# Branch gates by one tanh on ScalarE in place of exponential, addition and reciprocal, with the convolution tables copied in the input projections

## What is computed

```
h    = rms_norm(x) * (1 + scale) + shift
proj = h @ w_in                      # hy_u, hy_z, q, k, v, at_z, pl_u, pl_z, mg
y_hy = hyena_branch(hy_u) * silu(hy_z)       # 2 long convolutions, by DFT tables
y_at = diff_attention(q, k, v) * silu(at_z)  # 4 heads, 2 softmax maps in each
y_pl = pool_branch(pl_u) * silu(pl_z)
r    = sigmoid(mg)                   # 3 x 1024 channels
merged = r[0]*(y_hy @ w_hy_o) + r[1]*(y_at @ w_at_o) + r[2]*(y_pl @ w_pl_o)
x    = x + gate * (merged @ w_out)
```

## Time and profile before

| | us |
|---|---|
| median of three executions | 4487.88 |
| lowest, highest | 4482.55, 4494.41 |
| profiled execution, own time | 4486.91 |
| profiled execution, span of the core | 4485.2 |
| TensorE busy in the span | 3701.7 (83%) |
| VectorE busy | 2068.0 (46%) |
| ScalarE busy | 1068.8 (24%) |
| GpSimd busy | 775.1 (17%) |
| mean granted clock of TensorE | 0.913 |

### The profile page before, as it was taken

How to read it: one execution, slowest core, us unless ns; L and a number is a source line. 1 busy time by engine, 2 the same in 40 slices (tenths; PEclk the granted TensorE clock), 3 DMA queues, 4 the chain that set the end, 5 groups by cost and what they waited for, 6 DMA issues and landing times. The chain is left out here.

```text
span 4485.2 us, 53438 instructions
## 1 busy us (share of the span) xinstructions
PE 3701.7 (83%) x19456; PEld 3371.2 (75%) x19456; DVE 2068.0 (46%) x2294; ACT 1068.8 (24%) x1695; POOL 775.1 (17%) x390
## 2 busy tenths in 40 slices
PE   6988849997975877877998679988858787788999
PEld 6766639986764777777998679876647777778989
DVE  3444343222554676674333243234537667663332
ACT  1233321221111332332121121211113333331221
POOL 1112011220221111111111122202111111101211
PEclk9988969999887998999999889998879898899999
DMA  4656652212665221211333442125572122113334
GB/s 131 213 192 194 193 207 80 70 73 76 237 235 179 68 73 49 67 51 65 108 103 110 160 158 80 54 96 199 205 248 70 55 66 70 51 35 109 104 111 144
DMA packets 216869, 537.21 MB, mean 120 GB/s; under 512 B 37172, under 2 KB 78005, under 8 KB 215894
## 3 DMA queue, kind: packets, MB, share of 16 engines
q1 hardware_dynamic: 204214, 474.94, 31.3%
q10 hardware_dynamic: 12544, 60.82, 4.1%
HBM read 390.23 MB, written 165.17 MB: 124 GB/s over the span
## 5 line engine op out<-in xcount | busy, mean ns | idle before, releaser
L1753 PE MATMUL ps<-hh,attn_fwh 128*128 128x384 f32 x1152 | 430.2, 373 | 16.8 <-DMA hl<-h_keep 11.1
L1753 PE MATMUL ps<-hh,attn_fwl 128*128 128x384 f32 x1152 | 409.3, 355 | 0.0
L1753 PE MATMUL ps<-hl,attn_fwh 128*128 128x384 f32 x1152 | 408.0, 354 | 0.0
L2080 DVE RECIPROCAL attn_fout<-attn_fout 128x384 f32<-128x384 f32 x144 | 367.6, 2553 | 5.0
L1931 ACT ACTIVATE attn_prob<-ps,attn_nmax 128x1280 f32<-128x1280 f32 x144 | 176.0, 1222 | 527.4 <-DVE attn_nmax L2085 527.4
L127 PE MATMUL ps<-hh,mixin_wh 128*128 128x384 f32 x720 | 167.0, 340 | 102.3 <-POOL mixin_wl L1134 97.0
L1753 PEld LDWEIGHTS ps<-hh,attn_fwh 128*128 128x128 f32 x1152 | 233.3, 202 | 24.1 <-DMA hl<-h_keep 11.9
L1794 PE MATMUL ps<-ident,attn_prob 128*128 128x128 f32 x648 | 115.8, 294 | 161.2 <-DVE attn_wl L2105 91.8
L1753 PEld LDWEIGHTS ps<-hl,attn_fwh 128*128 128x128 f32 x1152 | 233.9, 203 | 0.0
L2007 POOL TENSOR_TENSOR attn_fwl<-attn_fraw,attn_fwh 128x1024 fp32r<-128x1024 f32 x48 | 121.4, 2530 | 649.0 <-ACT attn_fwh L1898 649.0
L1753 PEld LDWEIGHTS ps<-hh,attn_fwl 128*128 128x128 f32 x1152 | 232.6, 202 | 0.0
(11 more groups left out here) (264 smaller groups left out, 8762.7 us busy)
## 6 DMA issues: line engine op xcount, KB each, us to landing
gates<-attn_fout SPq DMA_DIRECT2D x144, 192.0 KB, 1.9
branch_gate<-gates SPq DMA_DIRECT2D x48, 576.0 KB, 3.8
H_dram<-fspec_hout SPq DMA_DIRECT2D x100, 256.0 KB
fspec_araw<-in_w_ada SPq DMA_DIRECT2D x48, 512.0 KB, 4.1
conv_hs<-H_dram SPq DMA_DIRECT2D x32, 768.0 KB, 5.6
attn_fraw<-in_w_mg ACTq DMA_DIRECT2D x48, 512.0 KB, 3.3
w_in_raw<-in_w_in SPq DMA_DIRECT2D x44, 512.0 KB, 3.9
fspec_draw<-in_dft_taps SPq DMA_DIRECT2D x68, 256.0 KB, 3.4
```

The lines of the kernel that those rows point to most:

```text
L1753: last = pe.matmul(ps[:, X_BANK, 0:CH], w[:, j % 2, k, :], x[:, k, (c % 3) * CH:(c % 3 + 1) * CH], start=(k == 0 and n == 0), stop=(k == K ...
L2080: dve.reciprocal(fout[:, c % 2], fout[:, c % 2]).then_inc(S["fr"], 1)
```

## The change

In attention `gate_out` computes tanh(x / 2) instead of exp(−x), and `sigmoid`, which made 1 / (1 + exp(−x)) of it, is gone from VectorE with its two semaphores; `store_gate` waits for ScalarE's activation. As sigmoid(x) = (1 + tanh(x / 2)) / 2, `branches_out` adds 1 to the gate in the same instruction that multiplies it with the product, and the factor of a half is put into the output stage's gate column.

The 32 table copies are taken out of the filters. `mixers_in` issues them from ScalarE's queue, two for each of 16 tiles: behind the eviction of tiles 0 to 11, and for the four pooling tiles directly behind `ready`. As `mixers_in` runs in each layer, there are 64 copies instead of 32. SyncE waits for them at the end of `mixers_in`, and `long_conv` no longer waits.

```diff
 def filters(...)
                         spectrum_out(m)
-                        if s % 2:
-                            i = n * 8 + s // 2
-                            name = ("dft_fwd", "dft_inv")[i // 16]
-                            act.dma_start(tables[name][i % 16], A[name][i % 16]).then_inc(s_tab, 16)
...
 def mixers_in(...)
                 sp.wait_ge(S["wv"], 16)
+                sp.wait_ge(S["tab"], 16 * 32)
...
+                def keep_table(i):
+                    for name in ("dft_fwd", "dft_inv"):
+                        act.dma_start(tables[name][i], A[name][i]).then_inc(S["tab"], 16)
...
                         evict_hy(2 * i + b, b)
+                        keep_table(2 * i + b)
                 for t in (10, 11):
                     ready(t)
                     split(t % 2, 6 * 16)
                     evict_hy(t, t % 2)
+                    keep_table(t)
...
                 for g in range(4):
                     ready(20 + g)
+                    keep_table(12 + g)
                     if g < 2:
                         split(g, 11 * 16)
...
 def long_conv(...)
-                sp.wait_ge(s_tab, 16 * 32)
...
 def attention(...)
                 def store_gate(h, c):
-                    sp.wait_ge(S["fr"], NCH * h + c + 1)
+                    sp.wait_ge(S["fev"], NCH * h + c + 2)
...
-                    nc.scalar.activation(fout[:, c % 2], ps[:, X_BANK, 0:CH], ACT.Exp, scale=-1.0).then_inc(S["fev"], 1)
+                    nc.scalar.activation(fout[:, c % 2], ps[:, X_BANK, 0:CH], ACT.Tanh, scale=0.5).then_inc(S["fev"], 1)
...
-                def sigmoid(h, c):
-                    q = NCH * h + c
-                    dve.wait_ge(S["fev"], q + 2)
-                    dve.tensor_scalar(fout[:, c % 2], fout[:, c % 2], 1.0, None, ALU.add).then_inc(S["fone"], 1)
-                    dve.wait_ge(S["fone"], q + 1)
-                    dve.reciprocal(fout[:, c % 2], fout[:, c % 2]).then_inc(S["fr"], 1)
...
                         low(h, u - 1, 0)
-                        sigmoid(h, cs[0])
                         maximum(h, u, 1)
                         low(h, u - 1, 1)
                         low(h, u - 1, 2)
                         combine(h, u)
-                        if u not in PV_OF:
-                            sigmoid(h, cs[1])
...
 def branches_out(...)
-                            dve.tensor_tensor(three(gate[:, b]), banks(b)[:, :, 0:CH], three(gate[:, b]),
-                                              ALU.mult).then_inc(S["p"], 1)
+                            dve.scalar_tensor_tensor(out=three(gate[:, b]), in0=three(gate[:, b]), scalar=1.0,
+                                                     in1=banks(b)[:, :, 0:CH], op0=ALU.add, op1=ALU.mult
+                                                     ).then_inc(S["p"], 1)
...
 def output(...)
-                        dve.tensor_copy(g, mod[:, bass.ds(2 * KD + m, 1), :].rearrange("p a n -> p (a n)")
-                                        ).then_inc(S["gc"], 1)
+                        dve.tensor_scalar(g, mod[:, bass.ds(2 * KD + m, 1), :].rearrange("p a n -> p (a n)"), 0.5, None,
+                                          ALU.mult).then_inc(S["gc"], 1)
```

More of the change, by code:

```diff
@@ L170, in build @@
         tables = {n: scratch(f"{n}_kept", [16, 2, P, BR]) for n in ("dft_fwd", "dft_inv")}
-        s_tab = top.enter_context(nc.semaphore("h_tab"))
         with phase(nc, "start") as ph:
@@ L182, in build @@
         mods = keep("mods", [P, DEPTH, 24, 2])
-        filters(nc, A, ps, mods, ident, x_state, H_dram, Hp_dram, hinv, tables, s_tab)
+        filters(nc, A, ps, mods, ident, x_state, H_dram, Hp_dram, hinv)
         with nc.Fori(0, DEPTH) as l:
@@ L192, in build @@
                 wv = hctx.enter_context(nc.sbuf_tensor("w_v_raw", [P, KD, BR], F32))
-                mixers_in(nc, A, l, ps, pr, ident, hh, hl, raw, wv, mix, qk)
+                mixers_in(nc, A, l, ps, pr, ident, hh, hl, raw, wv, mix, qk, tables)
                 values(nc, A, O, l, ps, hh, hl, wv, mix, v, vrows, s_kept)
             with nc.Fori(0, 2) as o:
-                long_conv(nc, A, l, o, ps, ident, v, mix, H_dram, Hp_dram, hinv, tables, s_tab)
+                long_conv(nc, A, l, o, ps, ident, v, mix, H_dram, Hp_dram, hinv, tables)
             vctx.close()
@@ L221, in reduce_and_sin, with filters @@
     return dve.tensor_scalar(ang, ang, PI_IN, -PI_IN, ALU.min, ALU.max)
-def filters(nc, A, ps, mods, ident, x_state, H_dram, Hp_dram, hinv, tables, s_tab):
+def filters(nc, A, ps, mods, ident, x_state, H_dram, Hp_dram, hinv):
     NU, NS = UNITS_F, TILES_F
@@ L877, with mixers_in @@
 WHY = NT + 4
-def mixers_in(nc, A, l, ps, pr, ident, hh, hl, raw, wv, mix, qk):
+def mixers_in(nc, A, l, ps, pr, ident, hh, hl, raw, wv, mix, qk, tables):
     with phase(nc, "mixin") as ph:
@@ L910, in mixers_in @@
                  "rot", "rused", "sp6", "spread", "qr", "cos", "sh0", "sh1", "pm", "pout", "pmm", "zero",
-                 "cw0", "cw1", "wv")
+                 "cw0", "cw1", "wv", "tab")
         S = {n: ph.sem(n) for n in names}
@@ L1287, in _, with long_conv @@
                     last.then_inc(s_mm, 1)
-def long_conv(nc, A, l, o, ps, ident, v, mix, H_dram, Hp_dram, hinv, tables, s_tab):
+def long_conv(nc, A, l, o, ps, ident, v, mix, H_dram, Hp_dram, hinv, tables):
     with phase(nc, "conv") as ph:
@@ L1604, in attention @@
                  "s", "max", "exp", "w", "tr", "wh", "wl", "pv", "o", "sum", "mean", "rt", "bc", "y",
-                 "st", "dve", "fw", "fhi", "flo", "fmm", "fev", "fone", "fr", "fst0", "fst1")
+                 "st", "dve", "fw", "fhi", "flo", "fmm", "fev", "fst0", "fst1")
         S = {n: ph.sem(n) for n in names}
@@ L2126, in body @@
                     split(h)
-                    a, b = STEP_CHUNKS[0]
-                    sigmoid(h, a)
                     maximum(h, 0, 0)
-                    sigmoid(h, b)
                     maximum(h, 0, 1)
@@ L2133, in body @@
                     for u in range(1, NU):
-                        cs = STEP_CHUNKS[u]
                         maximum(h, u, 0)
@@ L2145, in body @@
                         combine(h, u)
-                        if u not in PV_OF:
-                            sigmoid(h, cs[1])
-                    a, b, c = STEP_CHUNKS[NU]
                     scale(h, NPV - 3)
@@ L2151, in body @@
                     means(h, NPV - 2)
-                    sigmoid(h, a)
                     scale(h, NPV - 2)
-                    sigmoid(h, b)
                     means(h, NPV - 1)
                     scale(h, NPV - 1)
-                    sigmoid(h, c)
                 with dve.Fori(0, HEADS) as h:
```

## The result

The changed kernel takes 4202.70 us (median of four, 4191.75 to 4206.17) against 4491.15 before: a ratio of 0.9356, 95% interval 0.9334 to 0.9379. The profiled execution has a span of 4201.6 us, 283.6 less than before.

What follows compares the result with a forecast made beforehand. TensorE was taken to bound attention, standing still a fifth of the time behind VectorE's sigmoids. From 4486.91 us, −164 − 30 − 17 + 8 = −203 gave 4284 us; range for 8 in 10: 4205 to 4390.

Steps and rivals of the forecast that it cites:

- Attention's stops (−164): Attention, both layers: TensorE's waits shrink as sigmoids leave VectorE, 81.9 us a layer, −164 in all; bounds −112 and −194.
- the waits for `low`: Attention: TensorE's 40 waits for the weights' low part fall from 46.5 to 2 us a layer, −44.5.
- the head's start: Attention, heads 1 to 3: waits for the keys' low part fall from 24.6 to 10.2 us a layer, −14.4.
- the first weights: Attention: four waits for the first softmax weights fall from 16.5 to 7.6 us a layer, −8.9.
- the unnamed waits: Attention: TensorE's 16.8 us of waits with no releaser named shrink by 11.2 a layer; bounds 0 and −16.8.
- Those at the sums: Attention: TensorE's 10.8 us of waits at the sums stay, since `low` there follows ScalarE, not a sigmoid.
- Clock (−30): Attention: less time lost to the lower clock level, 3.75 us a head, −30 in all; bounds 0 and −79.
- Filters (−17): Filters: without copies holding SyncE's issues, 12 waits for `fspec_dl` shorten by 1.44 us each, −17; bounds 0 and −24.5.
- Input projections (+8): Input projections: added copies cost 4.1 us a layer, 3.1 of it at pooling tiles, +8; bounds 0 and +70.
- Rival 3: Input projections: the copies, two back to back, hold the stage, +70 in place of +8, 4346 us; chance 12%.
- Rival 4: Attention and filters: more comes back, clock −60 and filters −24.5, giving 4246 us; chance 13%.
- Rival 2: Attention: another chain, through ScalarE's cast, replaces the sigmoid; half the attention and clock gains stay away, 4381 us; chance 15%.

Runs made afterwards that it cites:

- dve_all: Changed kernel, with VectorE waiting for ScalarE's gate and running an unused 2.94 us instruction at all 18 old sigmoid places of a head: 4465.16 us.
- full_copies: Changed kernel plus 32 copies of 512 KB in the filters at their old places, into a scratch that nothing reads: 4241.41 us.
- small_copies: Changed kernel plus 32 copies of 16 KB in the filters at the old copies' places, into a scratch that nothing reads: 4196.08 us.
- keys_pool: Changed kernel with the keys' subtraction moved from GpSimd to VectorE and the pooling tiles' table copies put behind their evictions: 4161.27 us.
- keys_dve: Changed kernel with the subtraction for the keys' low part moved from GpSimd to VectorE: 4167.91 us.
- dve_split: Changed kernel with one unused VectorE instruction of 2.94 us ahead of the split of each head: 4211.44 us.

## Why the prediction was right in direction and short in size

The way and the cause were right; four terms were too small. Of the 81 us that the profiled execution gained beyond the forecast (284 against 203), some 32 are TensorE's standing still, 13 its clock, 19 a cost of every stop that had been put at nothing, and 22 the filters; the input projections take 8 of it back, and 3 us are not accounted for.

*Attention's stops (−164).* The mechanism held: with VectorE's time and wait put back at the 18 places (`dve_all`) the waits for `low` are 49.1 us again. The waits for `low`, the head's start, the first weights and the unnamed waits came out within 2.4 us a layer of their price, each. The step that failed is the one that left other waits as they were. Those at the sums were taken as bound by ScalarE; they fell from 10.8 to 4.3. Those for GpSimd's root behind the sums were counted among the waits "for data at its start", and fell to nothing. Before:

```profile
PE ps L1839 <- POOL attn_root L2015: 5.1, 4, 1.3
```

Both were late for the same reason as `low`: in `dve_all` they are back at 10.6 and 5.7. All standing still, window less busy time, fell by 96.4 and 99.7 us, 196 in all.

*Clock (−30).* This step failed twice. I took a little over a third of the loss by the clock as recovered, because mostly short stops were to go. By the trace's records of the clock TensorE was busy at the lower level for 76.6 us of layer 0 before and 31.9 after, 82.1 and 33.0 in layer 1: well over half of it went, 93.9 us. A gate matmul follows the one before in 0.32 us there (1662.97 to 1663.29 above) and in 0.17 at the upper level, so this is worth some 43 us. What remains of the long stops is 2.6 and 2.0 us, where they were 8.3 and 4.1. The other failure is a cost that was put at nothing: the last matmul ahead of a stop is busy for its whole 0.33 us, where otherwise the next one starts 0.17 us after its start (1657.86 and 1658.04 above). TensorE's waits in the two layers fell from 171 to 52 in number, and 119 times the 0.16 us that this adds is some 19 us. Together with the clock's 43 that is 62 of the 65 us (31.2 and 34.0) by which TensorE's busy time fell.

*Filters (−17).* The wait I had named for it gave 11.5 us and not 17; the stage gave 39. The hold on SyncE's queue was the right mechanism; the failed step is the bound of −24.5, the sum of the waits for `fspec_dl`. A held issue delays every load behind it on SyncE, and SyncE's issues took 45 us longer with the copies (`full_copies` against `small_copies`).

*Input projections (+8).* Measured +16 in the two profiled executions. In the eleven kernels that have the copies where the change put them, a layer takes 405.6 to 413.2 us, 410.1 in the mean; in the two without the copies 402.9 to 406.6, 405.1 in the mean. So it is 5 us a layer, 10 in all, and the rest is scatter: the term was right, and that the profiled pair shows 16 is chance. `keys_pool` (405.5 in the mean) points to the pooling tiles, as forecast; none of SyncE's issues there is over 1 us. Rival 3 is out.

*Rivals.* Rival 4, more comes back, is the nearest to what happened, but not by its own terms: the filters gave 39 us and not 24.5, the clock less than its 60, and the rest came from terms that it didn't have. Rival 2 had a true core: a chain through ScalarE is left (1.96 us of VectorE's idle time ahead of `low` in each step), but the waits for `low` are gone all the same. The lower end of the range doesn't follow from its words: rival 4 with the rest of its clock bound, 19 us, is 4227 and not 4205. Even 4205 left no room for all the stated bounds at once, which give 4189 (−194, −79, −24.5 and 0).

## What to carry to other kernels

Price a stop of the bounding engine at its idle time, at the tail of the matmul ahead of it and at the slow matmuls behind it: here 1.1 to 1.4 times the waits, and 1.8 in `keys_dve`, where the shorter stop left the clock at its upper level. Price work on a helper engine by the slack that is left ahead of the instruction that is waited for, and all moved instructions together: three that cost 57 us apart cost 76 together, in part by shared slack, in larger part by the clock. And price a background transfer by everything that stands behind the issue that it holds, not by the one wait that shows its name.

## What the runs showed of the hardware

VectorE instructions with all operands in SBUF took several times as long beside GpSimd's subtraction of the keys: one of 0.43 us took 4.63, one of 1.36 took 4.84. They ended 0.3 and 1.2 us behind GpSimd's. One that reads from PSUM, at 1656.44 in the kernel after, took 0.69 us in the middle of it, as it does elsewhere. GpSimd's own took 4.5 to 4.9 us in all heads before and after; at the head's start shown of `dve_split`, where a VectorE subtraction began at the same time, it took 5.74.

The row of the granted clock doesn't always tell the pace. In the first 104 us of the filters it reads 1.00 before and 0.67 after, but the same matmuls take the same time under both: three of 384 columns 1.33 us, sixty-four small ones 13.81. The trace before has no record of the clock ahead of 154 us, and the row reads 1.00 there; the trace after has its first at 37 us. So the mean over the span (0.913 before, 0.911 after) says nothing of what attention gained.
